# Fourier mixer with its norm and projection as one block, all products in three passes of high and low parts, its feature table loaded in the stage before

## The chip, the cores and the metric

The kernel runs on one core of a Trainium2 chip. The metric is the time of one execution on the device in microseconds (us); several executions are timed and the median counts. In the rows PE is TensorE's matmul, PEld its weight load, DVE is VectorE, ACT is ScalarE, POOL is GpSimd, and SPq is SyncE's DMA queue. All tensors are float32.

## The reference, cut to what matters

The reference is a three-layer network on 512 tokens (and 256 context tokens) of width 1024. In layer 1 the mixer is a Fourier transform over tokens and over groups of 256 features:

```python
def fourier_mix(h, w_f):
    b, n, d = h.shape
    hg = h.astype(jnp.float32).reshape(b, n, N_FOURIER_GROUPS, FOURIER_GROUP)
    f = jnp.fft.fft2(hg, axes=(1, 3), norm="ortho").real
    return f.reshape(b, n, d).astype(h.dtype) @ w_f
...
    x = x + 0.5 * mx[2] * swiglu(modulate(rms_norm(x, norm_g[i, 0]), mx[0], mx[1]), ffn1_w_gu[i], ffn1_w_d[i])
    hx = modulate(rms_norm(x, norm_g[i, 1]), mx[3], mx[4])
    x = x + mx[5] * fourier_mix(hx, fourier_w[f])
    x = x + 0.5 * mx[8] * swiglu(modulate(rms_norm(x, norm_g[i, 2]), mx[6], mx[7]), ffn2_w_gu[i], ffn2_w_d[i])
```

## The kernel before

The residual `xy` stays in SBUF with features on the partitions: 8 tiles of 128 features by 512 tokens. Weights pass through `ring`, three slots of 128x2048 floats (1 MB each), of which the feed-forward stages use slots 0 and 1. The network runs as a chain of blocks; each block has one instruction stream per engine, written out by hand, and ends for all engines together. Semaphore counts order the rest.

The part that the change rewrites stands between two calls of `feed_forward` (layer 1's ffn1 and ffn2). It is three things in two blocks:

- **norm** (L518): TensorE adds up squares (`sum_squares`, L269 and L272), ScalarE takes roots (L291), TensorE spreads them (`spread_roots`, L278 and L284), VectorE scales the 8 tiles (L551) and ScalarE shifts them (L536). The block also issues the loads of two tables, `dft_feature` (128x1024) and `dft_token` (128x4096) on the sync queue (L524).
- **fourier** (L1680): stage one multiplies each of 16 units (4 token tiles by 4 groups) by the feature table, 2 float32 matmuls of 128x512 each (L1696), and ScalarE and VectorE copy the results out in turn (L1715). Stage two makes 8 tiles of 8 float32 matmuls each with the token table (L1707), copied out in turn (L1718).
- **project_residual** (L1594): 8 tiles of 8 float32 matmuls (L1626) with `w_f`, two tiles for each 1 MB slab; VectorE adds them to the residual (L1651); ScalarE squares each new tile (`square_tile`, L254) and VectorE adds the square up (`add_square`, L259) for the next norm. One buffer holds the last square, so square and add alternate.

The other large stages, `feed_forward` and the first mixer among them, split each float32 operand in a high part, rounded to the float32r type (ScalarE), and a low part, the rest (VectorE, or GpSimd for the first slabs), and add three float32r matmuls: high by high, high by low, low by high (L715 to L717). `keep_busy` (L276) issues float32 matmuls of 128x128 whose result nobody reads. A float32 matmul leaves two records in the trace, a float32r matmul one.

## Time and profile before

| | us |
|---|---|
| median of 3 timed runs | 3352.56 (3350.9 to 3360.06) |
| profiled execution, device time | 3338.82 |
| its span, first to last instruction | 3336.7 |
| TensorE busy | 3079.3 (92%) |
| VectorE busy | 1376.8 (41%) |
| ScalarE busy | 846.4 (25%) |
| mean granted TensorE clock | 0.961 of full |

The profiled execution took 13.7 us less than the median of the timed ones, and it has about 2.1 us outside its span. Times in the trace count from the span's start. A row of the timeline reads: start, duration, engine, line, operation, output<-inputs, sizes, number of instructions merged, and in brackets how long the engine sat idle before it and who released it.

### The profile page before, as it was taken

To read this page: it belongs to the slowest core of one execution; us is meant where nothing else is said; L and a number is where in the kernel's file an instruction comes from. 1 tells how busy PE (TensorE), PEld (TensorE's weight loads), DVE (VectorE), ACT (ScalarE), POOL (GpSimd) and SP (SyncE) were. 2 spreads that over 40 slices of the span, in tenths; PEclk is the share of its full clock that TensorE was granted. 3 is DMA by queue.
4 is the path that set the end of the run, shared out by engine and by line. 5 is a ranking of instruction groups with operands and counts; after the bars stand their busy time and mean duration, and the time that the engine had idled before them with its cause. 6 is when DMAs were issued, how large, how long until landed. Compare 5 with 4: busy or idle time off the path is not lost. (4 is left out here: it accounts for less than half of the span.)

```text
span 3336.7 us, 37345 instructions
## 1 busy us (share of the span) xinstructions
PE 3079.3 (92%) x14686; PEld 2278.1 (68%) x14686; DVE 1376.8 (41%) x2137; ACT 846.4 (25%) x1333; POOL 243.9 (7%) x273
## 2 busy tenths in 40 slices
PE   6999999899788999999999999999999789878996
PEld 4888888777544787878888547888787554343334
DVE  4635454636565564653333213333411383221112
ACT  3111111332353321232222203222333261011111
POOL 1000000001000100010000001000100161012220
PEclk9999999999898999999999999999999799979997
DMA  6232323211001464632222102232222201338883
GB/s 243 104 125 94 134 83 125 91 51 52 12 1 37 163 242 144 239 116 101 88 101 81 64 26 100 82 107 87 90 101 77 84 1 38 149 147 339 347 349 123
DMA packets 78200, 395.19 MB, mean 118 GB/s; under 512 B 17536, under 2 KB 19968, under 8 KB 51712
## 3 DMA queue, kind: packets, MB, share of 16 engines
q1 hardware_dynamic: 66560, 385.12, 31.0%
q0 software_dynamic: 11520, 8.43, 0.8%
q8 instruction: 80, 1.31, 0.2%
q14 instruction: 40, 0.33, 0.0%
HBM read 443.82 MB, written 16.78 MB: 138 GB/s over the span
## 5 line engine op out<-in xcount | busy, mean ns | idle before, releaser
L715 PE MATMUL ps<-h_high_ffn,weights_high_ffn 128*128 128x512 f32 (+1 forms) x1696 | 624.7, 368 | 7.3 <-issue 3.8
L716 PE MATMUL ps<-h_low_ffn,weights_high_ffn 128*128 128x512 f32 (+1 forms) x1696 | 623.8, 368 | 0.0
L717 PE MATMUL ps<-h_high_ffn,weights_low_ffn 128*128 128x512 f32 (+1 forms) x1696 | 623.3, 368 | 0.0
L715 PEld LDWEIGHTS ps<-h_high_ffn,weights_high_ffn 128*128 128x128 f32 x1696 | 320.0, 189 | 62.3 <-issue 8.3
L717 PEld LDWEIGHTS ps<-h_high_ffn,weights_low_ffn 128*128 128x128 f32 x1696 | 319.9, 189 | 52.8
L716 PEld LDWEIGHTS ps<-h_low_ffn,weights_high_ffn 128*128 128x128 f32 x1696 | 320.1, 189 | 52.3
L715 PE MATMUL ps<-hidden_high_ffn,weights_high_ffn 128*128 128x512 f32 (+1 forms) x880 | 327.9, 373 | 19.3 <-DVE weights_low_ffn L850 12.1
L799 ACT ACTIVATE weights_high_ffn<-weights 128x2048 fp32r<-128x2048 f32 (+4 forms) x160 | 243.8, 1524 | 343.8 <-PE ps L717 275.6
L716 PE MATMUL ps<-hidden_low_ffn,weights_high_ffn 128*128 128x512 f32 (+1 forms) x880 | 326.4, 371 | 0.0
L717 PE MATMUL ps<-hidden_high_ffn,weights_low_ffn 128*128 128x512 f32 (+1 forms) x880 | 326.1, 371 | 0.0
L850 DVE TENSOR_TENSOR weights_low_ffn<-weights,weights_high_ffn 128x2048 fp32r<-128x2048 f32 (+4 forms) x160 | 289.6, 1810 | 82.5 <-ACT weights_high_ffn L799 80.9
L859 DVE TENSOR_TENSOR tmp<-ps,tmp 128x512 f32<-128x512 f32 x110 | 68.1, 636 | 429.1 <-ACT tmp L809 429.1
L809 ACT ACTIVATE tmp<-ps 128x512 f32<-128x512 f32 x110 | 58.6, 554 | 658.8 <-PE ps L717 655.1
L715 PEld LDWEIGHTS ps<-hidden_high_ffn,weights_high_ffn 128*128 128x128 f32 x880 | 167.3, 190 | 50.2 <-DVE weights_low_ffn L850 11.7
L716 PEld LDWEIGHTS ps<-hidden_low_ffn,weights_high_ffn 128*128 128x128 f32 x880 | 167.4, 190 | 28.0
L717 PEld LDWEIGHTS ps<-hidden_high_ffn,weights_low_ffn 128*128 128x128 f32 x880 | 167.1, 190 | 28.2
L874 DVE SCALAR_TENSOR_TENSOR xy<-ps,mods,xy 128x512 f32 (+1 forms) x112 | 72.6, 672 | 261.3 <-PE ps L717 261.1
L2679 PE MATMUL ps<-big,work 128*64 128x512 f32 x768 | 171.4, 598 | 6.5 <-issue 5.6
L373 DVE CUSTOM_DVE_ANT_0 scratch_ffn<-scratch_ffn 128x1024 f32<-128x1024 f32 x127 | 151.4, 1220 | 1.1 <-DMA scratch_ffn<-in_w_mod 1.1
L2679 PEld LDWEIGHTS ps<-big,work 128*64 128x64 f32 x768 | 65.7, 138 | 108.4 <-issue 108.4
L254 ACT ACTIVATE tmp<-xy 128x512 f32<-128x512 f32 (+3 forms) x64 | 43.8, 684 | 363.4 <-DVE xy L874 150.0
L320 POOL TENSOR_TENSOR weights_low_ffn<-weights,weights_high_ffn 128x512 fp32r<-128x512 f32 x32 | 43.0, 1362 | 1197.1 <-ACT weights_high_ffn L311 1196.9
(400 smaller groups left out, 4337.9 us busy)
## 6 DMA issues: line engine op xcount, KB each, us to landing
weights<-in_ffn_gu SPq DMA_DIRECT2D x88, 1024.0 KB, 4.9
big<-in_w_exp_gu SPq DMA_DIRECT2D x32, 2048.0 KB, 14.0
scratch_ffn<-in_w_mod SPq DMA_DIRECT2D x35, 1536.0 KB, 6.4
weights<-in_ffn_d SPq DMA_DIRECT2D x24, 768.0 KB, 4.2
weights<-in_w_in SPq DMA_DIRECT2D x16, 1024.0 KB, 4.8
weights<-in_ffn_d SPq DMA_DIRECT2D x24, 640.0 KB, 3.8
weights<-in_w_exp_dn SPq DMA_DIRECT2D x15, 1024.0 KB, 13.7
hbuf<-in_w_exp_dn SPq DMA_DIRECT2D x12, 1024.0 KB, 16.2
```

The lines of the kernel that those rows point to most:

```text
L254: scalar.activation(last_square[:, 0:cols], x, ACT.Square).then_inc(nm["squared"].sem, 1)
L320: gpsimd.tensor_tensor(quarter(w_low[:, s, :], c), quarter(ring.buf[:, s, :], c), quarter(w_high[:, s, :], c).bitcast(F32), ALU.subtract). ...
L373: vector.tensor_tensor_reduce(mod_w[b][:, j, :] if last else mod_product, mod_w[b][:, j, :], cond_row[:, c, :], 1.0, 0.0, ALU.mult, ALU.ad ...
L715: pe.matmul(out, wh, xh, start=(k == 0), stop=False)
L716: pe.matmul(out, wh, xl, start=False, stop=False)
L717: mm = pe.matmul(out, wl, xh, start=False, stop=(k == n - 1))
L799: scalar.activation(w_high[:, s, 0:n], ring.buf[:, s, 0:n], ACT.Copy).then_inc(high_done[s].sem, 1)
L809: scalar.activation(tmp[:, s, a:a + n], gate_up(s, 0, c), ACT.Silu).then_inc(silu_g[s].sem, 1)
L850: vector.tensor_tensor(w_low[:, s, 0:n], ring.buf[:, s, 0:n], w_high[:, s, 0:n].bitcast(F32), ALU.subtract).then_inc(ring.used[s], 1)
L859: vector.tensor_tensor(tmp[:, s, a:a + n], gate_up(s, 1, c), tmp[:, s, a:a + n], ALU.mult)\
L874: vector.scalar_tensor_tensor(x, down(s, c), g, x, ALU.mult, ALU.add)\
L2679: mm = pe.matmul(ps[b * CAP:(b + 1) * CAP, 2 + n % 2, :], gT[:, k, b * CAP:(b + 1) * CAP], w[:, k, :], start=(k == 0), stop=(k == KD - 1))
```

## The change

The norm, the transform and the projection become one block, `fourier_mixer`. All its products are done in three float32r passes. The feature table is loaded by the preceding feed-forward stage into ring slot 2; the token table is loaded at the start of the block. ScalarE makes all high parts (feature table, the 8 inputs, token table in four pieces, every result of stages one and two, the four slabs of `w_f`); VectorE makes the low parts, except those of the two tables, which GpSimd makes. Six PSUM banks rotate through stages one and two. The split weights have buffers of their own (the four slabs' low and high parts lie where tables and inputs lay), and the slabs `w_f[2]` and `w_f[3]` are requested when TensorE begins with slab 0 and slab 1. The first slab is multiplied with k outermost, so that it can begin before the last transformed tile is ready. Nine `keep_busy` matmuls are added after `spread_roots` and nine at the block's end.

```diff
+                        if table is not None:
+                            sync.dma_start(table[0], table[1].rearrange("p k n -> p (k n)")).then_inc(tables.sem, 16)
...
+            @block.sync
+            def _(sync):
+                sync.dma_start(cn, io["dft_token"].rearrange("p c t n -> p (c t) n")).then_inc(tables.sem, 16)
+                for n in range(2, 4):
+                    sync.wait_ge(ring.used[n % 2], n0[n % 2] + 1)
+                    sync.dma_start(ring.buf[:, n % 2, :], io["w_f"][n]).then_inc(ring.landed[n % 2], 16)
+                prefetch(sync, nxt, [n + 2 for n in n0])
+
+            @block.tensor
+            def _(pe):
+                def three(out, wh, wl, xh, xl, first, last):
+                    pe.matmul(out, wh, xh, start=first, stop=False)
+                    pe.matmul(out, wh, xl, start=False, stop=False)
+                    return pe.matmul(out, wl, xh, start=False, stop=last)
+
+                sum_squares(pe, NX)
+                spread_roots(pe, NX)
+                keep_busy(pe, 9)
+                pe.wait_ge(nm["early_low"].sem, l0 + 1)
+                for u in range(units):
+                    g, t = u // TT, u % TT
+                    tok = slice(t * P, (t + 1) * P)
+                    if t == 0:
+                        pe.wait_ge(in_low.sem, j0 + 2 * g + 2)
+                    if u >= 6:
+                        pe.wait_ge(low.sem, b0 + u - 5)
+                    for k in range(2):
+                        mm = three(ps[:, u % 6, :], h_high[:, 2 * g + k, tok], h_low[:, 2 * g + k, tok], cd_high[:, k, :],
+                                   cd_low[:, k, :], k == 0, k == 1)
+                    mm.then_inc(product.sem, 1)
+
+                pe.wait_ge(nm["early_low"].sem, l0 + 5)
+                for m in range(KD):
+                    g, half = m // 2, m % 2 * P
+                    pe.wait_ge(low.sem, b0 + max(TT * (g + 1), units + m - 5))
+                    for n in range(2 * TT):
+                        c, t = n // TT, n % TT
+                        a = slice(c * (C // 2) + half, c * (C // 2) + half + P)
+                        mm = three(ps[:, (units + m) % 6, :], Y_high[:, g, t, a], Y_low[:, g, t, a], cn_high[:, n, :],
+                                   cn_low[:, n, :], n == 0, n == 2 * TT - 1)
+                    mm.then_inc(product.sem, 1)
+
+                def out(m, k):
+                    n = m // 2
+                    at = slice((m % 2 * KD + k) * P, (m % 2 * KD + k + 1) * P)
+                    mm = three(ps[:, m % 4, :], w_high[n][:, at], w_low[n][:, at], F_high[:, k, :], F_low[:, k, :],
+                               k == 0, k == KD - 1)
+                    if k == KD - 1:
+                        mm.then_inc(fm["wo_product"].sem, 1)
+
+                for n in range(4):
+                    pe.wait_ge(fm["wo_low"].sem, k0 + n + 1)
+                    pe.sem_inc(ring.used[n % 2], 1)
+                    if n == 0:
+                        pe.wait_ge(low.sem, b0 + units + 6)
+                        for k in range(KD):
+                            pe.wait_ge(low.sem, b0 + units + k + 1)
+                            for m in range(2):
+                                out(m, k)
+                        continue
+                    for m in (2 * n, 2 * n + 1):
+                        if m >= 4:
+                            pe.wait_ge(fm["wo_added"].sem, r0 + m - 3)
+                        for k in range(KD):
+                            out(m, k)
+                keep_busy(pe, 9)
+
+            @block.scalar
+            def _(scalar):
+                def input_high(k):
+                    scalar.wait_ge(scaled.sem, z0 + k + 1)
+                    scalar.activation(h_high[:, k, :], full[:, k, :], ACT.Identity, bias=shift[:, k, 0:1])\
+                        .then_inc(in_high.sem, 1)
+
+                def evacuate(i):
+                    scalar.wait_ge(product.sem, p0 + i + 1)
+                    bank = ps[:, i % 6, :]
+                    if i < units:
+                        scalar.activation(Y_high[:, i // TT, i % TT, :], bank, ACT.Copy).then_inc(high.sem, 1)
+                    else:
+                        scalar.activation(F_high[:, i - units, :], bank, ACT.Copy).then_inc(high.sem, 1)
+
+                def token_table(c):
+                    scalar.activation(cn_high[:, 2 * c:2 * c + 2, :], cn[:, 2 * c:2 * c + 2, :], ACT.Copy)\
+                        .then_inc(nm["early_high"].sem, 1)
+
+                def w_split(n):
+                    scalar.wait_ge(ring.landed[n % 2], 16 * (n0[n % 2] + n // 2 + 1))
+                    scalar.activation(w_high[n], ring.buf[:, n % 2, :], ACT.Copy).then_inc(fm["wo_high"].sem, 1)
+
+                scalar.wait_ge(tables.sem, t0)
+                scalar.activation(cd_high.rearrange("p k n -> p (k n)"), feature_table, ACT.Copy).then_inc(nm["early_high"].sem, 1)
+                token_roots(scalar, NX)
+                for k in range(4):
+                    input_high(k)
+                for k in range(4, KD):
+                    evacuate(k - 4)
+                    input_high(k)
+                scalar.wait_ge(tables.sem, t0 + 16)
+                for i in range(4, units):
+                    evacuate(i)
+                    if i in (4, 6, 8, 10):
+                        token_table(i // 2 - 2)
+                scalar.wait_ge(nm["early_low"].sem, l0 + 1)
+                w_split(0)
+                for i in range(units, units + KD):
+                    evacuate(i)
+                for n in range(1, 4):
+                    w_split(n)
+                for m in range(KD):
+                    if m == KD - 1:
+                        scalar.activation(warm[:, 0:1], eps[:], ACT.Sqrt)
+                    scalar.wait_ge(fm["wo_added"].sem, r0 + m + 1)
+                    square_tile(scalar, m, xy[:, m, 0:NX], NX)
+
+            @block.gpsimd
+            def _(gpsimd):
+                gpsimd.wait_ge(nm["early_high"].sem, e0 + 1)
+                gpsimd.tensor_tensor(cd_low.rearrange("p k n -> p (k n)"), feature_table,
+                                     cd_high.rearrange("p k n -> p (k n)").bitcast(F32), ALU.subtract)\
+                    .then_inc(nm["early_low"].sem, 1)
+                for c in range(4):
+                    at = slice(2 * c, 2 * c + 2)
+                    gpsimd.wait_ge(nm["early_high"].sem, e0 + c + 2)
+                    gpsimd.tensor_tensor(cn_low[:, at, :], cn[:, at, :], cn_high[:, at, :].bitcast(F32), ALU.subtract)\
+                        .then_inc(nm["early_low"].sem, 1)
+
+            @block.vector
+            def _(vector):
+                def scale_in(k):
+                    vector.scalar_tensor_tensor(full[:, k, :], xy[:, k, 0:NX], gain[:, k, 0:1], spread_row(0), ALU.mult, ALU.mult)\
+                        .then_inc(scaled.sem, 1)
+
+                def input_low(k):
+                    vector.wait_ge(scaled.sem, z0 + k + 1)
+                    vector.wait_ge(in_high.sem, g0 + k + 1)
+                    vector.scalar_tensor_tensor(h_low[:, k, :], full[:, k, :], shift[:, k, 0:1], h_high[:, k, :].bitcast(F32),
+                                                ALU.add, ALU.subtract).then_inc(in_low.sem, 1)
+
+                def evacuate(i):
+                    vector.wait_ge(high.sem, a0 + i + 1)
+                    bank = ps[:, i % 6, :]
+                    if i < units:
+                        at = (slice(None), i // TT, i % TT, slice(None))
+                        vector.tensor_tensor(Y_low[at], bank, Y_high[at].bitcast(F32), ALU.subtract).then_inc(low.sem, 1)
+                    else:
+                        k = i - units
+                        vector.tensor_tensor(F_low[:, k, :], bank, F_high[:, k, :].bitcast(F32), ALU.subtract).then_inc(low.sem, 1)
+
+                def w_split(n):
+                    vector.wait_ge(fm["wo_high"].sem, h0 + n + 1)
+                    vector.tensor_tensor(w_low[n], ring.buf[:, n % 2, :], w_high[n].bitcast(F32), ALU.subtract)\
+                        .then_inc(fm["wo_low"].sem, 1)
+
+                def residual(m):
+                    vector.wait_ge(fm["wo_product"].sem, o0 + m + 1)
+                    vector.scalar_tensor_tensor(xy[:, m, 0:NX], ps[:, m % 4, :], gate[:, m, 0:1], xy[:, m, 0:NX],
+                                                ALU.mult, ALU.add).then_inc(fm["wo_added"].sem, 1)
+
+                invert_roots(vector, NX)
+                vector.wait_ge(nm["spread"].sem, nm["spread"].at + 1)
+                for k in range(KD + 1):
+                    if k < KD:
+                        scale_in(k)
+                    if k > 0:
+                        input_low(k - 1)
+                    if k >= 5:
+                        evacuate(k - 5)
+                for i in range(4, units):
+                    evacuate(i)
+                w_split(0)
+                clear_squares(vector, NX)
+                for i in range(units, units + KD):
+                    evacuate(i)
+                w_split(1)
+                w_split(2)
+                residual(0)
+                residual(1)
+                w_split(3)
+                for m in range(2, KD):
+                    residual(m)
+                    if m >= 4:
+                        add_square(vector, m - 4, NX)
+                for m in range(4, KD - 1):
+                    add_square(vector, m, NX)
+                vector.wait_ge(fm["wo_added"].sem, r0 + KD)
...
-    feed_forward("ffn1", 1, NX, mod_gain[1][:, 0], chunk(1, 0), chunk(1, 2), two(io["w_f"]))
-    own = stage_buffers("_1")
-    with nc.Block() as block:
-        norm(block, mod_gain[1][:, 1], chunk(1, 3),
-             [(dst, io[name], tables) for dst, name in zip(dft_tables(), ("dft_feature", "dft_token"))])
-    F = work[:, 0:KD * NX].rearrange("p (k n) -> p k n", k=KD)
-    with nc.Block() as block:
-        fourier(block, F)
-        project_residual(block, io["w_f"], F, chunk(1, 5), first_gu("ffn2", 1), raw_done)
-    own.close()
+    feed_forward("ffn1", 1, NX, mod_gain[1][:, 0], chunk(1, 0), chunk(1, 2), two(io["w_f"]), table=(feature_table, io["dft_feature"]))
+    fourier_mixer(first_gu("ffn2", 1))
```

The order of instructions shows it at three places. TensorE, between the end of the feed-forward stage and the Fourier stages, before (`big` and `hbuf` hold table and input; each row of 128x512 is one float32 matmul):

```order
4996 L278 MATMUL ps<-ident 128x128 x9
4997 L660 UNCONDITIONAL_BRANCH
4998 L540 UNCONDITIONAL_BRANCH
4999 L269 MATMUL ps<-ones,tmp 128x1 x4
5000 L272 MATMUL ps<-ones,tmp 128x1 x4
5001 L278 MATMUL ps<-ident 128x128 x3
5002 L284 MATMUL ps<-ident,inverse 128x128 x4
5003 L2854 UNCONDITIONAL_BRANCH
5004 L1687 UNCONDITIONAL_BRANCH
5005 L1696 MATMUL ps<-big,hbuf 128x512 x32
5006 L1707 MATMUL ps<-big 128x512 x64
```

And after:

```order
4999 L269 MATMUL ps<-ones,tmp 128x1 x4
5000 L272 MATMUL ps<-ones,tmp 128x1 x4
5001 L278 MATMUL ps<-ident 128x128 x3
5002 L284 MATMUL ps<-ident,inverse 128x128 x4
5003 L278 MATMUL ps<-ident 128x128 x9
5004 L1716 MATMUL ps<-dft_feature_high,fourier_h_high 128x512
5005 L1717 MATMUL ps<-dft_feature_low,fourier_h_high 128x512
5006 L1718 MATMUL ps<-dft_feature_high,fourier_h_low 128x512
```

Each float32 matmul has become three, the block boundary (the branch at L2854) is gone, and nine filler matmuls stand ahead of the first product.

ScalarE in stage one, after (L1783 takes the high part of a result out of PSUM, L1776 that of an input, L1788 that of a quarter of the token table; before, there were eight copies in a row here):

```order
553 L1776 ACTIVATE fourier_h_high<-fourier_input,mods 128x512
554 L1783 ACTIVATE fourier_high<-ps 128x512
555 L1776 ACTIVATE fourier_h_high<-fourier_input,mods 128x512
556 L1783 ACTIVATE fourier_high<-ps 128x512
557 L1788 ACTIVATE dft_token_high<-dft_token 128x1024
558 L1783 ACTIVATE fourier_high<-ps 128x512 x2
559 L1788 ACTIVATE dft_token_high<-dft_token 128x1024
560 L1783 ACTIVATE fourier_high<-ps 128x512 x2
561 L1788 ACTIVATE dft_token_high<-dft_token 128x1024
562 L1783 ACTIVATE fourier_high<-ps 128x512 x2
563 L1788 ACTIVATE dft_token_high<-dft_token 128x1024
```

The token table's four pieces stand between the results of stage one.

VectorE at the end of the projection, before (the last rows ahead of the block's end):

```order
1091 L1651 SCALAR_TENSOR_TENSOR xy<-ps,mods,xy 128x512
1092 L259 TENSOR_TENSOR tmp<-tmp 128x512
1093 L1651 SCALAR_TENSOR_TENSOR xy<-ps,mods,xy 128x512
1094 L259 TENSOR_TENSOR tmp<-tmp 128x512
1095 L1651 SCALAR_TENSOR_TENSOR xy<-ps,mods,xy 128x512
1096 L2858 UNCONDITIONAL_BRANCH
```

And after (L1861 is the residual, L1856 a slab's low part):

```order
1099 L1856 TENSOR_TENSOR fourier_w_low_11345<-weights,fourier_w_high_11341 128x2048
1100 L1861 SCALAR_TENSOR_TENSOR xy<-ps,mods,xy 128x512 x3
1101 L259 TENSOR_TENSOR tmp<-tmp 128x512
1102 L1861 SCALAR_TENSOR_TENSOR xy<-ps,mods,xy 128x512
1103 L259 TENSOR_TENSOR tmp<-tmp 128x512
1104 L1861 SCALAR_TENSOR_TENSOR xy<-ps,mods,xy 128x512
1105 L259 TENSOR_TENSOR tmp<-tmp 128x512
1106 L1861 SCALAR_TENSOR_TENSOR xy<-ps,mods,xy 128x512
1107 L259 TENSOR_TENSOR tmp<-tmp 128x512 x4
1108 L1704 UNCONDITIONAL_BRANCH
```

The adding of squares has moved back: four of the seven now stand behind the last residual, where none stood before.

## Rows read from the trace of the kernel before

**Rows 1.** The page: span, and busy time, share and instructions of TensorE.

```profile
span 3336.7 us, 37345 instructions
...
PE 3079.3 (92%) x14686; PEld 2278.1 (68%) x14686; DVE 1376.8 (41%) x2137; ACT 846.4 (25%) x1333; POOL 243.9 (7%) x273
```

**Rows 2.** Lines of 1500 to 2700 us: busy, mean ns | idle before, releaser.

```profile
L1626 PE MATMUL ps<-work,weights 128*128 128x512 f32 x128 | 55.9, 595 | 2.6 <-PE ps L1626 1.4 <-DVE work L1718 1.2
L1707 PE MATMUL ps<-big 128*128 128x512 f32 x128 | 55.2, 593 | 0.9 <-DVE big L1715 0.9
...
L1696 PE MATMUL ps<-big,hbuf 128*128 128x512 f32 x64 | 29.5, 625 | 6.6 <-PEq L2854 6.6
```

**Rows 3.** Timeline of TensorE, two passes of the feed-forward stage, 60 passes apart.

```profile
1840.88 0.39 PE L715 MATMUL ps<-hidden_high_ffn,weights_high_ffn 128*128 128x512 f32 x1
...
1854.48 0.39 PE L715 MATMUL ps<-hidden_high_ffn,weights_high_ffn 128*128 128x512 f32 x1
```

**Rows 4.** Timeline, the norm and the start of stage one.

```profile
1858.98 1.02 PE L269 MATMUL ps<-ones,tmp 128*128 128x1 f32 x8 [0.30 <-PEq L660]
...
1859.31 0.43 SPq L524 DMA_DIRECT2D big<-in_dft_token  x1
...
1864.17 5.36 DVE L551 SCALAR_TENSOR_TENSOR hbuf<-xy,mod_gain,ps 128x512 f32<-128x512 f32 x8 [2.72 <-PE ps L284]
...
1870.76 9.76 PE L1696 MATMUL ps<-big,hbuf 128*128 128x512 f32 x18 [6.62 <-PEq L2854]
```

**Rows 5.** Stretches: length, busy time of PE, PEld, DVE, ACT, POOL, granted clock, DMA share.

```profile
1868.00:1872.00 4.00, 1.24 (x2) 0.76 (x3) 1.52 (x3) 2.28 (x4) 0.00 (x0) 0.50 0.00 0
...
1876.00:1900.00 24.00, 24.00 (x57) 10.48 (x55) 4.84 (x7) 4.09 (x7) 0.00 (x0) 1.00 0.00 0
...
2018.00:2022.00 4.00, 3.35 (x16) 3.38 (x17) 0.00 (x0) 1.49 (x3) 2.49 (x2) 0.50 0.26 109
```

**Rows 6.** Timeline, the next feed-forward stage: input split and filler matmuls.

```profile
2025.18 3.52 PE L278 MATMUL ps<-ident 128*128 128x128 f32 x18
2025.43 1.41 DVE L908 SCALAR_TENSOR_TENSOR scratch_ffn<-xy,mod_gain,ps 128x512 f32<-128x512 f32 x2 [2.72 <-PE ps L284]
...
2027.04 0.75 DVE L914 SCALAR_TENSOR_TENSOR h_low_ffn<-scratch_ffn,mods,h_high_ffn 128x512 fp32r<-128x512 f32 x1 [0.20 <-ACT h_high_ffn L834]
...
2028.45 0.48 PE L751 MATMUL ps<-h_high_ffn,weights_high_ffn 128*128 128x512 f32 x1
```

**Rows 7.** Timeline, copies and splits of known size.

```profile
1510.61 1.90 ACT L799 ACTIVATE weights_high_ffn<-weights 128x2048 fp32r<-128x2048 f32 x1
...
1512.54 2.29 DVE L850 TENSOR_TENSOR weights_low_ffn<-weights,weights_high_ffn 128x2048 fp32r<-128x2048 f32 x1 [1.11 <-ACT weights_high_ffn L799]
...
1900.30 0.69 DVE L1715 COPY big<-ps 128x512 f32<-128x512 f32 x1 [2.74 <-PE ps L1696]
```

**Rows 8.** Timeline, GpSimd and VectorE splitting side by side in a feed-forward stage.

```profile
1498.71 0.73 DVE L908 SCALAR_TENSOR_TENSOR scratch_ffn<-xy,mod_gain,ps 128x512 f32<-128x512 f32 x1
...
1499.05 1.30 POOL L320 TENSOR_TENSOR weights_low_ffn<-weights,weights_high_ffn 128x512 fp32r<-128x512 f32 x1 [0.81 <-ACT weights_high_ffn L311]
...
1499.37 1.53 DVE L914 SCALAR_TENSOR_TENSOR h_low_ffn<-scratch_ffn,mods,h_high_ffn 128x512 fp32r<-128x512 f32 x1
```

**Rows 9.** DMA issues of the page: count, KB each, us to landing.

```profile
weights<-in_w_f SPq DMA_DIRECT2D x4, 1024.0 KB, 4.8
...
big<-in_dft_token SPq DMA_DIRECT2D x1, 2048.0 KB, 7.8
...
weights<-in_w_exp_dn SPq DMA_DIRECT2D x15, 1024.0 KB, 13.7
hbuf<-in_w_exp_dn SPq DMA_DIRECT2D x12, 1024.0 KB, 16.2
```

**Rows 10.** Timeline, end of the projection and start of the next stage.

```profile
2014.88 0.75 DVE L1651 SCALAR_TENSOR_TENSOR xy<-ps,mods,xy 128x512 f32<-128x512 f32 x1 [10.08 <-PE ps L1626]
...
2017.71 0.63 ACT L254 ACTIVATE tmp<-xy 128x512 f32<-128x512 f32 x1 [1.33 <-DVE xy L1651]
...
2018.65 1.84 PE L269 MATMUL ps<-ones,tmp 128*128 128x1 f32 x8 [3.81 <-PEq L2858]
```

**Rows 11.** Timeline, the kernel's start: squaring and adding alternate at 128x768.

```profile
13.37 0.84 ACT L254 ACTIVATE tmp<-xy 128x768 f32<-128x768 f32 x1 [1.02 <-DVE tmp L259]
...
14.24 0.96 DVE L259 TENSOR_TENSOR tmp<-tmp 128x768 f32<-128x768 f32 x1 [0.91 <-ACT tmp L254]
```

More of the change, by code:

```diff
@@ L237, in build @@
     y_read = [count(f"results_read{i}") for i in range(NX // P)]
-    fm = {n: count("first_" + n) for n in ("scaled", "in_high", "in_low", "w_high",
+    fm = {n: count(("mixer_" if n[:3] == "wo_" else "first_") + n) for n in ("scaled", "in_high", "in_low", "w_high",
         "w_low", "product", "evacuated", "head_summed", "head_swapped", "rows_rooted", "rows_ready", "head_turned",
@@ L590, in build, with feed_forward @@
     STREAMS = ((0, NX), (NX, NY))
-    def feed_forward(name, i, cols, gain, shift, gate, nxt, mod=None, rooted=False):
+    def feed_forward(name, i, cols, gain, shift, gate, nxt, mod=None, rooted=False, table=None):
         nonlocal mod_w, cond_row
@@ L923, in feed_forward @@
             normed(ns)
+        if table is not None:
+            tables.at += 16
         split_early()
@@ L1592, in first_mixer @@
             ring.n[s] += 2
+        for name, n in (("wo_high", 4), ("wo_low", 4), ("wo_product", KD), ("wo_added", KD)):
+            fm[name].at += n
     def project_residual(block, w, src, gate, nxt, ready, experts_ahead=False):
```

76 lines of the change are left out of this document (29 added, 47 removed).

## The prediction

> **What bounds the kernel now.** I read the page first: TensorE is busy for 92% of the span [rows 1], so what counts in a stage is what TensorE does there, and where it waits. Then the lines of the stretch that the change rewrites [rows 2]: three groups of float32 matmuls, 64, 128 and 128 records, busy 29.5, 55.2 and 55.9 us, each with little idle time before it except the first, 6.6 us. A float32 matmul is two records, so one product of 128x128 by 128x512 costs (55.2 / 64) 0.86 us. Third the timeline at the two ends [rows 4, 10]: the norm's first matmul starts at 1858.98, stage one at 1870.76, the last product is there at 2014.88 and the next stage's first matmul starts at 2018.65. That is 159.7 us from norm to norm, and TensorE computes in 140.6 of them.
>
> **The pace of a pass.** In the feed-forward stage, 60 float32r passes of the same shape lie between 1840.88 and 1854.48 [rows 3], so one is 0.2267 us and three are 0.68 us, against 0.86. The trace has this pace with the same split, the same width and the clock at full. I take it for all 480 passes: 96 in stage one (16 units by 2 by 3), 192 in stage two (8 by 8 by 3), 192 in the projection.
>
> **Start.** Up to the spread roots nothing changes for TensorE. ScalarE gets the feature table's high part before the roots, some 1.0 us (half of 1.90 [rows 7]); it can start at the block's start, about 0.3 us ahead of 1858.98, and must be free some 2 us later, when the sums are there: cost nothing. VectorE can scale from 1864.17 [rows 4]. Before, TensorE waited for all 8 tiles, for the shift and for the block's end, until 1870.76. Now it waits for two tiles with both parts. The next stage has that chain [rows 6]: scaling begins at 2025.43, the first low part at 2027.04, then a scaling and a low part come in steps of some 0.66 to 0.75; the second low part is ready about 3.7 us after the chain's start. So the first pass is at 1864.2 + 3.7 = 1867.9, 2.9 us earlier. The nine new filler matmuls take 3.52 us at half clock [rows 6], from about 1864.0 to 1867.6: just hidden. In the next stage the fillers run the same way and the first pass behind them takes 0.48 [rows 6], no half-pace time. I therefore take full clock from the first pass. The other end is what happened here before, where half clock stood at the first matmuls [rows 5]: about 4 us at half pace loses some 2 us. Bounds of the start: a gain of 2.9, down to 0.9.
>
> **Stage one.** 96 x 0.2267 = 21.8 us against 29.5 [rows 2]: 7.7 less, ending at 1889.7. Can the others follow? A unit lasts 1.36 us; ScalarE's high part of a result is about 0.63 and VectorE's low part about 0.69 [rows 7, 10], so both have half of it free. The first four results come while inputs 4 to 7 are still being split; there VectorE needs 0.73 + 0.75 + 0.69 = 2.2 us for each tile, and TensorE eats a pair of tiles in 5.44. VectorE is through with result 3 near 1878.3, and unit 9 needs its bank at 1880.1. No wait; a slip of 1 us is possible.
>
> **The token table's gate.** Stage two now also waits for GpSimd's four low parts. The table is requested at the block's start and lands 7.8 us later [rows 9], near 1867, early enough. ScalarE splits piece 0 after result 4, which I place at 1876.7 by its queue, so the piece is ready at 1877.8; pieces 1 to 3 follow by 1884.8. GpSimd took 1.30 us for 512 columns [rows 8], 2.6 to 2.7 for 1024 in the range that page and row allow, so four pieces end at 1877.8 + 4 x 2.7 = 1888.6, 1.1 us before TensorE asks. This is the thinnest cover in the change. If GpSimd and VectorE get in each other's way it goes. The trace shows how [rows 8]: VectorE's low part, which reads two tensors in SBUF, took 1.53 us beside a GpSimd split instead of 0.75, while the scaling ahead of it, which reads one in SBUF and one in PSUM, kept 0.73. The low parts of results read PSUM and one SBUF tensor and are of the second kind. The Trainium skill says the same as a rule (SBUF — State Buffer, "Who interferes with whom"): a VectorE instruction with at most one SBUF input doesn't contend with GpSimd, one with two does, and then the later of the two fully blocks. By that rule the gate costs nothing; if the rule failed here, some eight low parts of 0.69 would be queued into GpSimd's chain, and stage two would start about 4.4 us late. Range of the gate: 0 to 4.4; I take 0.
>
> **Stage two.** 192 x 0.2267 = 43.5 against 55.2, and the 0.9 us wait for the last copies goes [rows 2], since tile 0 needs 11 results and they are there: 12.6 less. It ends near 1933.2. A tile takes 5.44 us, and its two copies 1.3.
>
> **Projection.** 43.5 against 55.9, and the idle 2.6 us [rows 2] go: 15.0 less. What could take their place: slab 0 is split during stage two. Its first seven k steps need tiles that are done, and they last 9.5 us, which covers the last tile's copies. Slab 1 needs its split (1.90 + 2.29 [rows 7]) after these copies: ready near 1938.8, wanted at 1944. Slab 2 is requested when TensorE begins slab 0, 1933.2, lands after 4.8 [rows 9] and is split by 1943; wanted at 1955. Slab 3: requested 1944, split by 1953.5, wanted at 1966. VectorE stands still for slab 3's high part with residual 2 queued behind it; tile 6 needs that residual's bank only at 1966. All hidden. TensorE's last pass ends at 1867.9 + 480 x 0.2267 + 0.2 = 1976.9, where it was 2014.8: **37.9 us earlier**.
>
> **The tail.** Here the change gives something back. Before, the last product at 2014.88 was followed by 3.46 us (residual, square, add, residual, square, up to 2018.34 [rows 10]). Now additions 3 to 6 stand behind the last residual, and one buffer makes square and add alternate. The kernel's start shows the alternation [rows 11]: 0.84 and 0.96 with 0.06 between. At 512 columns a square is 0.63 and an addition 0.69. So: residual 0.75, add 0.69, four squares 2.52, three adds 2.07, eight handovers 0.5: 6.5 us. That is **3.0 us more**, and it is on the path, since the next norm needs the sum. TensorE's nine fillers cover 2.2 to 3.5 of it, then it idles 3 to 4 us as it did before (3.81 [rows 10]); the next norm ran at half clock [rows 5], and I leave it so. Were the clock full there, up to 1.6 us would be gained.
>
> **Feature table in the stage before.** A 512 KB load between two slab loads on the sync queue, in a stage where ScalarE takes the slab at 1510.61 without a wait [rows 7]. By half the time of a 1 MB slab it is some 2.4 us of the queues, against slabs wanted every 10.9 us (48 passes). Cost nothing; 0 to 2.
>
> **Sum.** 2.9 + 7.7 + 12.6 + 15.0, less 0.3 for rounding and the last drain, is 37.9; less 3.0 is 34.9 us. The profiled execution becomes 3338.8 - 34.9 = 3303.9. The timed median stood 13.7 above the profiled execution, so against the median: 3352.56 - 34.9 = **3317.7**. With the bounds together (start -2, stage one -1, gate -4.4, table -2; clock +1.6) the gain is between 25.5 and 36.5.
>
> **Rivals.**
> *A: the thin covers fail.* Half clock at the start, the gate late by its full 4.4, and some input waits in stage one: the gain is 20 to 28, time near 3328. For it: the gate's margin is 1.1 us on a chain of ten instructions; half clock did stand at this start before. Against: the first pass behind the same fillers [rows 6]. Chance 0.12.
> *B: the slab loads become the bound, slower than before.* Slabs 2 and 3 are asked for only when TensorE reaches slabs 0 and 1, 21.8 us before they are wanted, and 4.2 of that is splitting. A landing of 17.6 us is hidden; each us beyond it shows. The time would be lost altogether only with landings of about 35 us each, which gives 3353 or more; at 40 us, some 3360. For it: landings of 1 MB up to 16.2 in the experts' stage. Against: those share the queues with other loads, and w_f took 4.8 [rows 9]. Chance 0.02.
> *C: the passes don't run at the feed-forward's pace*, because here both operands change from pass to pass in other layouts, or the clock is held down with them. At 0.27 us a pass 480 of them take 20.8 more: 3339. The stationary tiles are 128 contiguous columns as there. Chance 0.04.
> *D: the gain is there and the stages behind take it back* (their loads or GpSimd work have a time of their own). Every later stage begins after a block's end for all engines, so it moves whole. Within 0.3%: chance 0.03.
>
> **Numbers.** The forecast keeps 0.79. About 0.3%, 10 us, is what a measurement of this kernel can tell from no change. Faster by more 0.94, within 0.03, slower 0.03 (B and the slow end of C). The range holds the forecast's bounds and A; the medians add a few us of their own, since executions of the same kernel lie between 3338.8 and 3360.1: 3305 to 3333.
>
> **What the profile of after would show.** The first pass some 9 us after the norm's first matmul; no idle time before stage two's first pass, with GpSimd's last low part about 1 us ahead of it; 96, 192 and 192 passes 0.227 apart; ScalarE's high part of slab 3 done well before TensorE's slab 2 ends; four additions alternating with squares behind the last residual, 6.5 us; the distance from norm to norm 124.8 us. I am wrong if that distance is right and the rest of the kernel has grown, or if the passes come further apart.

## The result

The changed kernel took 3307.49 us (median of 4 runs, 3304.18 to 3321.24) against 3351.73 of the kernel before (4 runs); the ratio is 0.9877, 95% interval 0.9846 to 0.9909. Timed again in a later session, beside 11 runs of the kernel before, it was 0.9913 (0.9881 to 0.9944). The forecast, 34.9 us or a ratio of 0.9896, lies between the two and inside both intervals. The profiled execution took 3304.18 us, where 3303.9 had been forecast, and the median 3307.49, where 3317.7 had been. That the first agrees within 0.3 us is luck, since the four runs spread over 17 us.

First the page of after, span and TensorE, which answers to [rows 1]:

```profile
span 3302.0 us, 37776 instructions
...
PE 3051.4 (92%) x14882; PEld 2309.7 (70%) x14882; DVE 1398.5 (42%) x2161; ACT 865.2 (26%) x1354; POOL 255.9 (8%) x278
```

TensorE is busy for 27.9 us less and still for 92% of the span: what the change took was mostly TensorE's own work. Next the lines of 1500 to 2700 us, to set beside [rows 2] (one of each three passes; the other two have the same busy time within 0.1 us):

```profile
L1716 PE MATMUL ps<-dft_token_high,fourier_high 128*128 128x512 f32 x64 | 24.9, 389 | 0.0
L1716 PE MATMUL ps<-fourier_out_high,fourier_w_high 128*128 128x512 f32 x64 | 24.9, 389 | 0.0
...
L1716 PE MATMUL ps<-dft_feature_high,fourier_h_high 128*128 128x512 f32 x32 | 12.5, 392 | 1.7 <-DVE fourier_h_low L1841 1.7
```

The only idle time of the whole block's products is 1.7 us ahead of the first. Passes overlap, so busy times of the three groups can't be added; the timeline gives the distances. It shows the start of the block, the change from stage one to stage two, and the end:

```profile
1858.28 1.02 PE L269 MATMUL ps<-ones,tmp 128*128 128x1 f32 x8 [0.30 <-PEq L660]
...
1863.11 2.40 PE L278 MATMUL ps<-ident 128*128 128x128 f32 x18
1867.18 0.47 PE L1716 MATMUL ps<-dft_feature_high,fourier_h_high 128*128 128x512 f32 x1 [1.68 <-DVE fourier_h_low L1841]
...
1884.05 2.40 POOL L1829 TENSOR_TENSOR dft_token_low<-dft_token,dft_token_high 128x1024 fp32r<-128x1024 f32 x1 [0.32 <-ACT dft_token_high L1788]
...
1889.03 0.39 PE L1716 MATMUL ps<-dft_token_high,fourier_high 128*128 128x512 f32 x1
...
1976.28 0.75 DVE L1861 SCALAR_TENSOR_TENSOR xy<-ps,mods,xy 128x512 f32<-128x512 f32 x1 [4.10 <-PE ps L1718]
1976.94 0.68 DVE L259 TENSOR_TENSOR tmp<-tmp 128x512 f32<-128x512 f32 x1
1978.38 0.69 DVE L259 TENSOR_TENSOR tmp<-tmp 128x512 f32<-128x512 f32 x1 [0.76 <-ACT tmp L254]
...
1982.06 0.63 ACT L254 ACTIVATE tmp<-xy 128x512 f32<-128x512 f32 x1 [0.73 <-DVE tmp L259]
...
1982.99 1.80 PE L269 MATMUL ps<-ones,tmp 128*128 128x1 f32 x8 [4.75 <-PEq L1704]
```

From the norm's first matmul (1858.28) to the next norm's (1982.99) it is 124.71 us, where it was 159.67 [rows 4, 10]. Stage one's 96 passes last 21.85 us, stages two and three 43.5 each. The last residual, four additions alternating with squares, and the last square take 6.41 us. The 4.75 us in brackets in the last row are TensorE's wait for them.

In the table, all distances are differences of two rows' starts in the timelines of one execution each; "first pass" counts from the norm's first matmul (L269), "behind" runs from the next norm's first matmul to the end of the span.

| kernel | norm's place | first pass | stage one | norm to norm | next norm to its stage's first pass | behind |
|---|---|---|---|---|---|---|
| before | 1858.98 | 11.78 | 30.4 | 159.67 | 9.80 | 1318.0 |
| after | 1858.28 | 8.90 | 21.85 | 124.71 | 9.25 | 1319.0 |
| after, second profile | 1869.93 | 7.76 | 21.86 | 123.59 | 9.81 | 1318.5 |

(Stage one of before includes the 0.9 us wait behind it.) The two profiles of the changed kernel differ by 10 us in span, 3302.0 and 3312.0, and none of that is in the block: the norm stands 11.7 us later, and the norm at the end of the first mixer already 10.4 (1108.16 and 1118.53). That much of the spread of the runs was made ahead of the block.

Inside the block the two differ by 1.1 us, at the first pass. The granted clock is at half (1.2 GHz) for a while in both, but not at the same place. The rows give the length, TensorE's busy time, the granted clock, and the share and GB/s of the DMA; they are of the changed kernel, of its second profile, and of a timed variant from below (squares early):

```profile
1861.00:1863.00 2.00, 2.00 (x11) 0.50 0.95 410
...
1873.50:1875.50 2.00, 2.00 (x11) 0.50 1.03 442
...
1871.00:1873.00 2.00, 2.00 (x6) 0.50 0.03 8
```

In the first the half clock falls on the norm's own matmuls (the three fillers inside `spread_roots` take 1.55 us), in the second on the nine fillers behind them (those three take 0.91 us, the nine 3.60 instead of 2.40), in the third on stage one's passes. In the profile of before it falls on the norm's matmuls too (1.63 us), so the first profile is the one to compare it with. What decides the place is not shown.

The stages behind the block took nothing back: 1318.0 us before, 1319.0 and 1318.5 after. Rival D falls.

### The profile page after: what moved, and what is told of

Read it like the earlier page. It is cut to its first block and busy times, and to the rows that moved or that the text cites. A ratio compares the mean times of both kernels' runs of the same rounds, so it can differ in the third digit from the quotient of the medians.

```text
span 3302.0 us, 37776 instructions
## 1 busy us (share of the span) xinstructions
PE 3051.4 (92%) x14882; PEld 2309.7 (70%) x14882; DVE 1398.5 (42%) x2161; ACT 865.2 (26%) x1354; POOL 255.9 (8%) x278
## 5 line engine op out<-in xcount | busy, mean ns | idle before, releaser
L254 ACT ACTIVATE tmp<-xy 128x512 f32<-128x512 f32 (+3 forms) x64 | 43.7, 684 | 331.8 <-DVE xy L876 149.9
```

Source lines behind the costliest of these rows:

```text
L254: scalar.activation(last_square[:, 0:cols], x, ACT.Square).then_inc(nm["squared"].sem, 1)
```

## The experiments

All are edits of the changed kernel, and all but the timed ones are read by their distances in one profile. What they are compared with is the pair of profiles above: 124.71 and 123.59 us from norm to norm.

**Float32 passes in the new block.** The one product:

```diff
-                    pe.matmul(out, wh, xh, start=first, stop=False)
-                    pe.matmul(out, wh, xl, start=False, stop=False)
-                    return pe.matmul(out, wl, xh, start=False, stop=last)
+                    return pe.matmul(out, wh.bitcast(F32), xh.bitcast(F32), start=first, stop=last)
```

> The new block with one float32 matmul in place of each three float32r passes: it multiplies the high parts alone, so the low parts' share of the result is left out; all splits, waits, buffers and fillers stay. My theory (the gain is TensorE's pace plus the waits at the stage boundaries): 160 float32 matmuls at 0.86 us are 137.6 us against 108.8 for the 480 passes, so the distance from the norm's first matmul to the next norm's first matmul grows from 124.7 to about 153.5 us, still 6 us under the 159.7 of the kernel before. Rival (most of the gain comes from running as one block, with splits hidden, and the passes themselves bring little): the distance stays under 135 us.

Measured: norm to norm 152.20 us (1866.63 to 2018.83), 27.5 more than after and 7.5 less than before. The first pass stands 7.87 us behind the norm, as in the second profile; against that one the edit costs 28.6 us. Its lines of the block:

```profile
L1716 PE MATMUL ps<-dft_token_high,fourier_high 128*128 128x512 f32 x128 | 55.1, 592 | 0.0
L1716 PE MATMUL ps<-fourier_out_high,fourier_w_high 128*128 128x512 f32 x128 | 55.1, 592 | 0.0
L1716 PE MATMUL ps<-dft_feature_high,fourier_h_high 128*128 128x512 f32 x64 | 27.7, 593 | 0.6 <-DVE fourier_h_low L1839 0.6
```

The busy time of [rows 2] is back, except that stage one takes 27.7 us and not 29.5: it starts at full clock here. The idle time is not back. So of the 35.0 us between the norms 27.5 are the passes' pace (of 36.1 in the second profile, 28.6), and 7.5 the block's form: less waiting and 1.8 us of clock in stage one, net of what the tail gives back. The pace is the main cause, and the rival that it brings little falls.

**Squares added early.** VectorE's order in the projection:

```diff
                 w_split(3)
-                for m in range(2, KD):
-                    residual(m)
-                    if m >= 4:
-                        add_square(vector, m - 4, NX)
-                for m in range(4, KD - 1):
-                    add_square(vector, m, NX)
+                residual(2)
+                add_square(vector, 0, NX)
+                add_square(vector, 1, NX)
+                residual(3)
+                add_square(vector, 2, NX)
+                add_square(vector, 3, NX)
+                for m in range(4, KD):
+                    residual(m)
+                    if m < KD - 1:
+                        add_square(vector, m, NX)
```

> The squares of finished tiles are added right behind their residual (tiles 0 and 1 behind residual 2, tiles 2 and 3 behind residual 3, then one each), so only residual 7 and square 7 stand behind the last product. Theory (the tail is on the path and is the alternation of square and add): the 6.4 us from the last residual's start to the last square's end shrink to 1.4, the distance from norm to norm is 119.7 us, 5.0 less, and the time falls by 5 us. If the clock stays at full for the next norm because TensorE's fillers now reach up to it, another 1.5 us come off behind it. Rival (the tail is hidden behind TensorE's fillers or the block's end): no more than 2 us come off.

Measured: 119.40 us, and 7.04 us behind it. Its timeline at the end:

```profile
1983.26 0.75 DVE L1861 SCALAR_TENSOR_TENSOR xy<-ps,mods,xy 128x512 f32<-128x512 f32 x1 [3.30 <-PE ps L1718]
...
1984.05 0.63 ACT L254 ACTIVATE tmp<-xy 128x512 f32<-128x512 f32 x1 [4.72 <-DVE xy L1861]
...
1985.53 1.02 PE L269 MATMUL ps<-ones,tmp 128*128 128x1 f32 x8 [0.30 <-PEq L1704]
...
1992.57 0.47 PE L753 MATMUL ps<-h_high_ffn,weights_high_ffn 128*128 128x512 f32 x1
```

Residual and square take 1.4 us where 6.4 stood, and from the end of the last pass to the next norm it is 2.30 us instead of 6.75. TensorE's fillers now reach the next norm (idle 0.30 instead of 4.75), the norm's eight matmuls take 1.02 and not 1.80 us, and the next stage starts another 2.2 to 2.8 us sooner. The tail was on the path, and it cost more than its own length.

**Without the nine fillers ahead of stage one.**

```diff
                 spread_roots(pe, NX)
-                keep_busy(pe, 9)
```

> The nine filler matmuls between the spread roots and stage one are taken out. Theory (they are hidden behind VectorE's first splits and hold the clock): the first pass starts at the same 8.9 us behind the norm's first matmul, but the granted clock is at half for the first passes, as it was at stage one of the kernel before; about 4 us at half pace lose 2 us, so norm to norm is about 126.7 us. Rival (the fillers do nothing, or cost something): norm to norm stays 124.7 or is shorter.

Measured: the first pass 8.24 us behind the norm, stage one 24.09 us instead of 21.85, norm to norm 126.29. The stretches show why (length, busy time of PE, PEld, DVE, ACT, POOL, granted clock, DMA share), of this kernel and then of after:

```profile
1871.00:1875.00 4.00, 0.14 (x1) 0.17 (x2) 3.76 (x6) 2.10 (x3) 0.00 (x0) 0.50 0.55 233
1875.00:1879.00 4.00, 4.00 (x10) 3.13 (x11) 3.02 (x5) 1.92 (x3) 0.00 (x0) 0.50 0.02 4
```

```profile
1867.00:1871.00 4.00, 3.81 (x17) 3.21 (x18) 4.00 (x8) 2.88 (x6) 0.00 (x0) 1.00 0.02 4
```

10 passes in 4 us at half clock (1.2 GHz), against 17 from a start inside the stretch at full clock (2.4 GHz). The fillers save 2.2 us of stage one here. They do not always: see the timed runs.

**Without the nine fillers at the end.**

```diff
                         for k in range(KD):
                             out(m, k)
-                keep_busy(pe, 9)
```

> The nine filler matmuls at the block's end are taken out. With them TensorE still sits idle for 4.75 us and the next norm runs at half clock. Theory (they end too early to matter): norm to norm 124.7 us as with them, and the next norm's first matmul to the next stage's first pass 9.3 us as with them. Rival (they hold the clock): that stretch grows by 1 us or more.

Measured: norm to norm 123.81 us, and 9.60 us to the next first pass, between the 9.25 and 9.81 of the two profiles with them. TensorE now idles 6.76 us, and it runs the next norm at half clock either way (1.84 and 1.80 us). As the changed kernel stands, these nine are worth nothing; with the squares early they end 0.30 us ahead of the next norm (that kernel was not run without them).

**GpSimd's work doubled.**

```diff
+                    if c > 0:
+                        gpsimd.wait_ge(nm["early_low"].sem, l0 + c + 1)
+                    gpsimd.tensor_tensor(waste, cn[:, at, :], cn_high[:, at, :].bitcast(F32), ALU.subtract)\
+                        .then_inc(spent.sem, 1)
+                    gpsimd.wait_ge(spent.sem, c + 1)
                     gpsimd.tensor_tensor(cn_low[:, at, :], cn[:, at, :], cn_high[:, at, :].bitcast(F32), ALU.subtract)\
```

> GpSimd makes each low part of the token table twice, once into a buffer nobody reads, so its work behind stage one doubles; the result is the same. In the changed kernel its last low part is ready 28.2 us after the norm's first matmul and stage two begins at 30.7. Theory (stage two waits for the slower of TensorE and GpSimd, cover 2.6 us): eight pieces of 2.40 us end 18.2 + 19.2 + some 0.3 of handovers = 37.7 us after the norm's first matmul, stage two starts there, some 7 us late, and norm to norm is about 131.5 us. VectorE's low part of slab 0, with two inputs in SBUF, falls beside GpSimd's work and takes longer than 2.29 us; the low parts of results, with one, keep 0.69. Rival (the pieces are needed one after another, so much of it is hidden, or VectorE and GpSimd share without loss): under 3 us more and 2.29 us for that slab.

Measured: stage two starts 39.14 us behind the norm, 8.4 later than in the first profile, and norm to norm is 135.43 us, more than either theory had. The timeline and a stretch:

```profile
1900.87 2.34 POOL L1832 TENSOR_TENSOR waste<-dft_token,dft_token_high 128x1024 f32<-128x1024 f32 x1
1903.29 4.27 POOL L1835 TENSOR_TENSOR dft_token_low<-dft_token,dft_token_high 128x1024 fp32r<-128x1024 f32 x1
...
1899.24 0.69 DVE L1855 TENSOR_TENSOR fourier_low<-ps,fourier_high 128x512 fp32r<-128x512 f32 x1 [0.67 <-ACT fourier_high L1784]
1901.04 4.32 DVE L1862 TENSOR_TENSOR fourier_w_low<-weights,fourier_w_high 128x2048 fp32r<-128x2048 f32 x1 [1.11 <-ACT fourier_w_high L1794]
...
1907.61 0.79 PE L1717 MATMUL ps<-dft_token_high,fourier_high 128*128 128x512 f32 x1 [9.03 <-POOL dft_token_low L1835]
```

```profile
1908.00:1912.00 4.00, 4.00 (x10) 3.08 (x10) 0.00 (x0) 0.00 (x0) 0.00 (x0) 0.50 0.00 0
```

Three things add up. GpSimd's eight pieces gate stage two, as the theory said. On top of that VectorE's split of slab 0, two inputs in SBUF, met GpSimd: it started at 1901.04, in GpSimd's piece that ran to 1903.2, took 4.32 us instead of 2.29, and ended at 1905.36; GpSimd's next piece, begun at 1903.29, took 4.27 instead of 2.4. Each stood still for about as long as the other needed. The low parts of results, one input in SBUF, kept 0.69 beside GpSimd. The Trainium skill (SBUF — State Buffer, "Who interferes with whom") has it as a rule: a VectorE instruction with at most one SBUF input does not contend with GpSimd, one with two contends with a GpSimd instruction that reads SBUF, and the shared ports are an exclusive lock. This trace agrees: 0.69 beside GpSimd for the one kind, 4.32 for 2.29 for the other. The third is the clock: after 9.03 us of idle time TensorE starts at half, and stage two takes 45.84 us instead of 43.5.

**The feature table loaded in the block.**

```diff
             def _(sync):
+                sync.dma_start(feature_table, io["dft_feature"].rearrange("p k n -> p (k n)")).then_inc(landed.sem, 16)
                 sync.dma_start(cn, io["dft_token"].rearrange("p c t n -> p (c t) n")).then_inc(tables.sem, 16)
...
-                scalar.wait_ge(tables.sem, t0)
+                scalar.wait_ge(landed.sem, 16)
```

(The load in the feed-forward stage is taken out.)

> The feature table is loaded at the start of the Fourier block, ahead of the token table, and not in the stage before. Theory: ScalarE's high part of it waits for the load (request near 0.0 us of the norm's first matmul, 3.3 us to landing as it had in the kernel before), and the roots stand behind it on ScalarE; they start at about 4.4 us and not at 1.95, so the whole block moves by 2.5 us and norm to norm is 127.2 us. Nothing changes in the feed-forward stage before. Rival (the early load costs the feed-forward stage as much as it brings here): norm to norm 127.2, but the feed-forward stage before is shorter by 1 us or more. Second rival (the load is hidden here as well): norm to norm 124.7.

Measured: the first pass 10.77 us behind the norm, norm to norm 126.61. ScalarE:

```profile
1871.88 1.06 ACT L1794 ACTIVATE dft_feature_high<-weights 128x1024 fp32r<-128x1024 f32 x1 [4.20 <-DMA weights<-in_dft_feature]
1872.84 0.25 ACT L291 ACTIVATE inverse<-ps,eps 128x4 f32<-128x4 f32 x1
```

The roots stand behind the table and start 4.3 us after the norm's first matmul (1868.53) instead of 1.95. The early load is worth 1.9 to 3.0 us, by which of the two profiles one takes. The feed-forward stage ahead is 370.24 us from its norm to the next, with the load (1488.04 to 1858.28) and without it (1498.29 to 1868.53), and 370.23 in the kernel before: there the load costs nothing.

**The first slab tile by tile.**

```diff
-                        for k in range(KD):
-                            pe.wait_ge(low.sem, b0 + units + k + 1)
-                            for m in range(2):
+                        for m in range(2):
+                            for k in range(KD):
+                                if m == 0:
+                                    pe.wait_ge(low.sem, b0 + units + k + 1)
                                 out(m, k)
```

> The projection's first slab is multiplied tile by tile and not with k outermost. Theory: tile 0 reaches its last k 4.8 us into the projection, and the last transformed tile is split 1.6 us into it, so the order is worth nothing here: norm to norm 124.7 us, within 0.9 of the changed kernel. Rival (the order hides the last split): 1 us or more is lost at the start of the projection.

Measured: norm to norm 124.49 us, no idle time in the projection, which takes 43.7 us from first pass to last end, as in both profiles of the changed kernel. The order of the loops is worth nothing here.

**The slabs requested late.**

```diff
-                    pe.sem_inc(ring.used[n % 2], 1)
+                    if n > 0:
+                        pe.wait_ge(fm["wo_product"].sem, o0 + 2 * n)
+                        pe.sem_inc(ring.used[(n - 1) % 2], 1)
...
+                pe.wait_ge(fm["wo_product"].sem, o0 + KD)
+                pe.sem_inc(ring.used[1], 1)
```

(The last increments also free the slots for the next stage's first slabs, so those are requested late too.)

> Slabs 2 and 3 of the projection's weights are requested only when the last product of slab 0, and of slab 1, is there, 11 to 15 us later than in the changed kernel; TensorE waits for that product each time. Theory (landing 4.8, high part 1.9 and low part 2.3 us add up to 9.0, and a slab lasts 10.9): the loads stay hidden, and only the three waits cost, 0.3 to 0.8 us each, so norm to norm is 125.6 to 127 us. Rival (slab loads near the bound): TensorE waits for the low parts of slabs 2 and 3, 3 us or more in all.

Measured: norm to norm 126.02 us; the projection takes 44.84 us from first pass to last end where it took 43.7. ScalarE waits for both slabs:

```profile
1956.92 1.92 ACT L1797 ACTIVATE fourier_w_high<-weights 128x2048 fp32r<-128x2048 f32 x1 [13.52 <-DMA weights<-in_w_f]
1969.11 1.92 ACT L1797 ACTIVATE fourier_w_high<-weights 128x2048 fp32r<-128x2048 f32 x1 [10.27 <-DMA weights<-in_w_f]
```

The two slabs were requested 11.1 and 22.4 us behind the projection's first pass, where the changed kernel requested them 4.0 us ahead of it and 6.9 behind. With 15 us of cover taken away from each load, 1.1 us is lost. TensorE loses the same 0.35 us at all three slab boundaries, also at the first, whose slab had long been split, so the waits for products account for it; the low parts of slabs 2 and 3 were ready 2.0 and 1.1 us before TensorE took them. The next stage still takes 375.4 us from norm to norm. Rival B, the slab loads as the bound, is far away.

**The timed kernels.**

> The changed kernel itself, timed beside the kernel before. Theory (all of the gain is the 35.0 us between the two norms and 0.5 behind it; the remaining spread of the times lies in other stages and has nothing to do with the change): ratio 0.9893, within 0.002, and norm to norm 124.7 us, within 0.9. Rival (the change also speeds up or slows down the rest): a ratio of 0.987 or below, or 0.992 or above.

> The kernel with the squares added early, timed. Its one profile showed norm to norm 119.4 us and the next stage's first pass 7.0 us behind it instead of 9.3, 7.5 us in all. Theory: 7.5 us under the changed kernel, a ratio to before of 0.9871. Rival (given back in the stages behind): the ratio of the changed kernel.

The third has the squares early, and takes the input's wait inside the loop over k:

```diff
-                    if t == 0:
-                        pe.wait_ge(in_low.sem, j0 + 2 * g + 2)
...
                     for k in range(2):
+                        if t == 0:
+                            pe.wait_ge(in_low.sem, j0 + 2 * g + k + 1)
```

> Squares added early, and stage one's first unit of each group waits for its two input tiles one by one, so its first three passes can start when one tile is split. Theory: the second tile is split 1.3 us behind the first, three passes take 0.7, so 0.7 us come off the distance from norm to norm: 118.7 to 119.0 us, and the first pass starts within 7 to 8 us of the norm. In the time this can't be told from the kernel without it: ratio 0.987. Rival (a wait more in TensorE's queue, and the clock falls at an earlier start): no gain or 1 us lost.

| kernel | median of 6, us | ratio to before, 95% interval | first pass | stage one | norm to norm | next first pass |
|---|---|---|---|---|---|---|
| after | 3319.86 | 0.9913 (0.9881 to 0.9944) | 7.76 | 21.86 | 123.59 | 9.81 |
| squares early | 3303.89 | 0.9863 (0.9836 to 0.9891) | 7.51 | 23.46 | 120.48 | 6.34 |
| and input by k | 3304.55 | 0.9861 (0.9832 to 0.9891) | 7.03 | 22.1 | 118.65 | 6.33 |

Both variants have a lower median than the changed kernel; against the median of before they save 45.1 and 44.5 us. From the norm to the next stage's first pass the profiles of the early squares have 126.4 and 126.8 us, those of after 134.0 and 133.4, so 6.6 to 7.5 less. The medians differ by 16, with intervals that just overlap: what is beyond the 7.5 can't be put down to the edit, and the changed kernel's own median moved by 12 between the two sessions (3307.49 and 3319.86). The wait by k is worth less than these times can tell, and 0.75 us from norm to norm against the first profile of the early squares (119.40). The row of squares early has one surprise, stage one at 23.46 us. In that execution the nine fillers ahead ran at full clock and ended early, and TensorE idled 1.86 us:

```profile
1865.92 2.17 PE L278 MATMUL ps<-ident 128*128 128x128 f32 x18
1869.96 0.47 PE L1716 MATMUL ps<-dft_feature_high,fourier_h_high 128*128 128x512 f32 x1 [1.86 <-DVE fourier_h_low L1841]
...
1870.88 0.63 PE L1716 MATMUL ps<-dft_feature_high,fourier_h_high 128*128 128x512 f32 x1
```

The clock fell behind the second pass and was back at 1874: 1.6 us lost.

## Why the prediction was right, step by step

- **Pace.** 0.2267 us a pass: 43.52 us for 192 (1889.03 to 1932.55). Exact, since the rows of the feed-forward stage had the same shape and split [rows 3]. Rival C falls. The float32 experiment confirms the step by itself: 27.5 us (28.6 against the second profile) where the sum has 28.8 for pace.
- **Start.** Forecast 8.9 us behind the norm, measured 8.90, and 7.76 in the second profile. The chain was right: TensorE waits for the second tile's low part. The fillers' length was off in the first profile: 2.40 us, not 3.52, so they were not "just hidden" but ended 1.7 us early, since the clock was back at full for most of them. In the second they took 3.60 us at mostly half clock and ended 0.48 us ahead, nearly as forecast. The forecast had one clock for each step, and the place of the half clock moves between executions. Full clock from the first pass held in both profiles of the changed kernel, but not in the timed variant above, where 1.6 us of the bound of 2 were lost; so it is partly luck.
- **Stage one.** 21.85 against 21.8. The low part of result 3, forecast near 1878.3, came before that: VectorE takes four results in one go from 1876.02 on, and TensorE waited for no bank.
- **The gate.** Cover 1.1 us forecast, 2.6 measured: GpSimd's last piece ended at 1886.45, stage two started at 1889.03. GpSimd took 2.40 us for 1024 columns, and I had doubled and rounded up the row for 512. The chain was also another than the forecast's four pieces back to back: GpSimd sat idle for 0.32 us ahead of the last piece, until ScalarE's fourth high part was there (row 1884.05 above), and that one stands behind result 10 in ScalarE's queue and so moves with TensorE. Wherever the first pass fell, the cover stayed 2.57 or 2.58 us, in nine profiles of the changed kernel and of the edits that leave the passes and GpSimd's work as they are. The main part of rival A, the thin covers, falls with it. The step that weighed the port was right in both directions: the low parts kept 0.69 us beside GpSimd, and doubling the work shows what a crossing with the other kind costs.
- **Stage two and projection.** No idle time, as forecast. Slab 2 was requested at 1928.57, 4 us before TensorE's array reached slab 0; the queue ran ahead of the array, which the forecast had left out. It was cover that nobody needed.
- **Tail.** 6.5 us forecast, 6.41 measured. Giving back 3.0 of the gain was right: from the last pass's end to the next norm it is 3.8 us before and 6.75 after. The forecast left the norm behind it at half clock, as before, and allowed up to 1.6 us for a full one. That was too little: with the squares early the next stage's first pass comes 2.2 to 2.8 us sooner behind the norm.
- **The next stage.** Assumed unchanged at 9.80; it was 9.25 and 9.81.
- **Feature table in the stage before.** Cost forecast at 0 to 2, taken at 0; it is 0.00 (370.23 and 370.24).
- **Against the median.** The sum was 34.9. Between the norms it is 34.96, and 36.1 with the second profile. The two timings say 44 and 29, and lie to both sides of the sum. Single executions differ by more than that in stages that the change leaves alone: over all profiles of the changed kernel and its edits the norm stands anywhere from 1858 to 1872 us, the norm at the end of the first mixer already anywhere from 1108 to 1119, and the stretch behind the block's last norm took 1317.0 and 1323.9 us in two profiles of one and the same kernel (squares early). What makes them differ the runs here do not settle. The kernel before has only one profile, so how much its own 159.67 us vary is not known.

## What to carry to other kernels

Three passes in the rounded type are 0.68 us where a float32 product is 0.86, and the gain is all there only if every split hides beside TensorE; list each split with the time at which it is ready and the time at which it is wanted, and the smallest difference is the place to watch. Look at what is queued behind the last product: work that could have run earlier, left in a queue for order's sake, is paid in full, and here once more in the clock of what follows. And when two executions of one kernel differ by more than the change, compare distances between fixed places of the trace, not spans.

## What the runs showed of the hardware

- Idle gaps of 1.68 us (the changed kernel) and 1.79 us (slabs requested late) ahead of the first pass left the clock at full; one of 1.86 us (squares early, timed) was followed by half clock 0.9 us into the passes, with the same fillers ahead.
- With the same instructions, half clock fell on the norm's matmuls in one execution, on the fillers in a second and, with the squares early, on the first passes in a third.
- Behind 3.87 us of idle time the first passes ran at half from the start, and so did the norm's matmuls behind 4.75 and 6.76 us.
- VectorE and GpSimd, each with a split of two SBUF tensors, stood still for each other in turn: 4.32 us for 2.29 and 4.27 for 2.40.
